# Expert results by indirect DMA to a table of rows, instead of a scatter on TensorE for each expert

## The reference

```python
N_EXPERTS, TOP_K, D_FF_EXPERT = 8, 2, 2816
logits = xt @ router
top_val, top_idx = lax.top_k(logits, TOP_K)
top_w = jax.nn.softmax(top_val, axis=-1)
gates = sum(one_hot(top_idx) * top_w)             # (tokens, experts)
for e in range(N_EXPERTS):
    out = out + gates[:, e:e + 1] * ((silu(xt @ wg[e]) * (xt @ wu[e])) @ wd[e])
x = layer_norm(ALPHA * x + out, ln2_g, ln2_b)
```

## Time and profile before

| | |
|---|---|
| Median of 3 runs | 2399.91 us (2394.61 to 2399.92) |
| The profiled execution, whole | 2399.19 us |
| Its span, first to last instruction | 2397.4 us |
| TensorE busy (matmuls) | 2368.5 us, 99% |
| DVE busy | 1722.4 us, 72% |
| ACT busy | 1450.2 us, 60% |
| GpSimd (POOL) busy | 80.4 us, 3% |
| HBM read, written | 551.10 MB, 1.05 MB |
| Mean granted TensorE clock | 0.999 of full |

### The profile page before, as it was taken

How to read it: one execution, slowest core, us unless ns; L and a number is a source line. 1 busy time by engine, 2 the same in 40 slices (tenths; PEclk the granted TensorE clock), 3 DMA queues, 4 the chain that set the end, 5 groups by cost and what they waited for, 6 DMA issues and landing times. The chain is left out here.

```text
span 2397.4 us, 31585 instructions
## 1 busy us (share of the span) xinstructions
PE 2368.5 (99%) x12354; PEld 1993.1 (83%) x12354; DVE 1722.4 (72%) x1921; ACT 1450.2 (60%) x1674; POOL 80.4 (3%) x114
## 2 busy tenths in 40 slices
PE   9999999999999999999999999999999999999998
PEld 7889978788888888888878788888888888887887
DVE  5665466899898899889986755666656766568565
ACT  6454454688888888888856544454444544456442
POOL 0000010000000000000001100000000000003000
PEclk9999999999999999999999999999999999999999
DMA  8255552699999999899955355443555255453552
GB/s 314 94 198 204 189 202 75 262 366 361 352 361 357 344 366 371 338 358 363 359 192 206 129 207 185 180 177 116 207 186 194 87 191 191 186 189 124 189 190 104
DMA packets 81806, 555.18 MB, mean 232 GB/s; under 512 B 11072, under 2 KB 11840, under 8 KB 16192
## 3 DMA queue, kind: packets, MB, share of 16 engines
q1 hardware_dynamic: 81600, 552.19, 61.7%
HBM read 551.10 MB, written 1.05 MB: 230 GB/s over the span
## 5 line engine op out<-in xcount | busy, mean ns | idle before, releaser
L2140 DVE TENSOR_TENSOR wlo<-raw,whi 128x2048 fp32r<-128x2048 f32 x484 | 1105.3, 2295 | 432.7 <-ACT whi L1690 431.6
L1690 ACT ACTIVATE whi<-raw 128x2048 fp32r<-128x2048 f32 x487 | 932.6, 1928 | 538.5 <-PE bank L896 139.0
L818 PE MATMUL bank<-whi,xt 128*128 128x512 f32 (+1 forms) x1056 | 311.1, 379 | 2.4 <-DVE xt L2157 1.3
L1237 PE MATMUL bank<-whi,xt 128*128 128x512 f32 (+1 forms) x768 | 222.4, 374 | 1.5 <-DVE e_hf L2786 1.4
L818 PEld LDWEIGHTS bank<-whi,xt 128*128 128x128 f32 x1056 | 189.4, 188 | 39.9 <-issue 3.3
L1052 PE MATMUL bank<-xt,whi 128*128 128x512 f32 x768 | 209.1, 394 | 0.0
L818 PE MATMUL bank<-wlo,xt 128*128 128x512 f32 (+1 forms) x528 | 197.6, 374 | 0.0
L896 PE MATMUL bank<-whi,h_hi 128*128 128x512 f32 x596 | 184.9, 391 | 0.0
L896 PE MATMUL bank<-whi,h_lo 128*128 128x512 f32 x596 | 183.9, 390 | 0.0
L896 PE MATMUL bank<-wlo,h_hi 128*128 128x512 f32 x596 | 183.8, 390 | 0.0
L1237 PEld LDWEIGHTS bank<-whi,xt 128*128 128x128 f32 x768 | 138.5, 188 | 26.4 <-DVE e_hf L2786 1.9
(11 more groups left out here) (346 smaller groups left out, 3700.6 us busy)
## 6 DMA issues: line engine op xcount, KB each, us to landing
raw<-in_units SPq DMA_DIRECT2D x509, 1024.0 KB, 5.0
gain<-in_ln_g SPq DMA_DIRECT2D x4, 512.0 KB, 6.8
gain<-in_ln_b SPq DMA_DIRECT2D x4, 512.0 KB, 8.5
gain<-in_attn_norm_g SPq DMA_DIRECT2D x4, 512.0 KB, 6.0
gain<-in_mlp_norm_g SPq DMA_DIRECT2D x4, 512.0 KB, 6.1
toep<-in_toeplitz SPq DMA_DIRECT2D x2, 768.0 KB, 10.0
cst<-in_cst SPq DMA_DIRECT2D x1, 1120.0 KB, 18.9
x<-in_x SPq DMA_DIRECT2D x4, 256.0 KB, 6.0
```

The source lines that it names most:

```text
L818: mm = pe.matmul(proj_bank(l, c, t)[:, 0:width], a[:, kx, t * P:(t + 1) * P], b[:, k, :], start=(kx == 0 and i == 0), stop=(kx == KT - 1 a ...
L1237: mm = pe.matmul(bank[b][:, 0:width], a[:, kx, :], w[:, k, :], start=(kx == 0 and i == 0), stop=(kx == KT - 1 and i == 2))
L1690: act.activation(whi[u % NH][:, :], raw[u % NR][:, :], ACT.Copy).then_inc(hi_ready[u % NR], 2)
L2140: dve.tensor_tensor(wlo[u % NR][:, :], raw[u % NR][:, :], whi[u % NH][:, :].bitcast(F32), ALU.subtract).then_inc(lo_ready[u % NR], 2)
```

## The change

The results of experts 0 to 6 are no longer scattered by a matmul. ACT copies the four result banks to a plain float32 tile (`give_plain_result`; `xt_rows` and `odd_rows` lie on the same bytes as `xt` and the odd token tiles), and GpSimd issues two indirect DMAs an expert, one for each tile of 128 slots. They write slot rows of 4 KB to a table `rows` in HBM: row 2 x token + choice, where choice is 1 if the expert is the token's second. Slots without a token get an index of at least 1024, past the bounds, and are not written. `index_rows` on TensorE finds the row of each slot: four matmuls of the permutation with `row_base` (eight columns), in place of `turn_perm`; DVE adds 1024 and casts (`index_of_rows`). In the last expert, before the loads of group 45, SyncE waits until all stores have landed and reads the table back, 1 MB for each tile of tokens; DVE combines the two rows of each token with their softmax weights in groups 3 and 4 (`add_rows`, three instructions a tile), in place of the single add in group 2. The last expert keeps its scatter. An all-zero input `no_rows` is copied to the table in layer 0, after the small loads. `y` is no longer cleared.

```diff
+            xt_rows = sb("xt_rows", [P, 2, 2, D], scope=plain)
+                odd_rows = sb("odd_rows", [P, 2, 2, D], scope=plain)
@@ SyncE, load_experts and layer 0
+                    if g == n - NG + 3:
+                        sp.wait_ge(rows_stored, 32 * (N_EXP - 1))
+                        back = rows.rearrange("(t p w) d -> t p w d", t=NT, w=2)
+                        for t in range(NT):
+                            sp.dma_start(rows_of(t), back[t]).then_inc(rows_back, 16)
                     if g < n:
                         load_units(PLAN.gate[1][g])
...
                     small()
+                    sp.dma_start(rows, A["no_rows"]).then_inc(rows_cleared, 16)
@@ GpSimd
-                            pool.memset(y[:, t, half * 512:(half + 1) * 512], 0.0).then_inc(added, 1)
+                    pool.wait_ge(rows_cleared, 16)
+                    for e in range(N_EXP - 1):
+                        pool.wait_ge(map_ready, e + 1)
+                        pool.wait_ge(ye_hi_ready, 4 * e + 4)
+                        for st in range(NT):
+                            pool.indirect_dma_start(
+                                rows, bass.IndirectOffsetOnAxis(ap=row_of[:, e, st:st + 1], axis=0),
+                                plain_results(e)[:, st], None, bounds_check=2 * S - 1,
+                                oob_is_err=False).then_inc(rows_stored, 16)
@@ TensorE
+            def index_rows(e):
+                third_bank_free(e)
+                if e < 2:
+                    pe.wait_ge(wide_placed, e + 1)
+                for st in range(NT):
+                    for t in range(NT):
+                        mm = pe.matmul(bank[3][:, st * 8:(st + 1) * 8], perm[:, e // 2 % 2, t, st, e % 2], row_base[:, t],
+                                       start=(t == 0), stop=(t == 1))
+                mm.then_inc(slots_mapped, 1)
...
                 def between(i, place):
-                    if i == 1 and place == 0 and e:
-                        narrow_or_wide(n_before, scatter, e - 1)
                     if i == 2 and place == 0:
-                        turn_perm(e)
+                        (index_rows if n_next is not None else turn_perm)(e)
...
                         if g == 1:
-                            pe.wait_ge(perm_t_ready, e + 1)
+                            pe.wait_ge(map_ready, e + 1)
...
+                        if n_next is not None:
+                            pe.wait_ge(map_ready, e + 1)
                         next_own(gate_of, 0)
@@ ACT
                 def take_tokens(p, g):
                     act.wait_ge(gathered, p * 8 + (g + 1))
+                    if p and g == 4:
+                        act.wait_ge(rows_stored, 32 * (2 * p - 1))
...
+                def give_plain_result(e):
+                    wait_used(act, PLAN.down[1][e * NG + NG - 1][-1])
+                    if e:
+                        act.wait_ge(rows_stored, 32 * e)
+                    for b in range(4):
+                        act.activation(plain_results(e)[:, b // 2, b % 2 * 512:(b % 2 + 1) * 512], bank[4 + b][:, :],
+                                       ACT.Copy).then_inc(ye_hi_ready, 1)
@@ DVE
+                def index_of_rows(e):
+                    dve.wait_ge(slots_mapped, e + 1)
+                    dve.tensor_scalar(row_of[:, e], bank[3][:, 0:16].rearrange("p (s e) -> p s e", s=NT)[:, :, e],
+                                      float(NO_ROW), None, ALU.add).then_inc(map_ready, 1)
+                def add_rows(t):
+                    dve.wait_ge(rows_back, 32)
+                    link(dve.tensor_scalar(y[:, t], rows_of(t)[:, 0], topf[:, t, 6:7], None, ALU.mult))
+                    link(dve.scalar_tensor_tensor(out=y[:, t], in0=rows_of(t)[:, 1], scalar=topf[:, t, 7:8],
+                                                  in1=y[:, t], op0=ALU.mult, op1=ALU.add))
+                    link(dve.scalar_tensor_tensor(out=x[:, t], in0=x[:, t], scalar=ALPHA, in1=y[:, t], op0=ALU.mult,
+                                                  op1=ALU.add))
...
+                for t in range(NT):
+                    dve.tensor_scalar(row_base[:, t], cst[:, C_IOTA:C_IOTA + 8], topf[:, t, 1:2],
+                                      cst[:, C_ROW + t:C_ROW + t + 1], ALU.is_equal, ALU.add)
                 for e in range(2):
                     place_tokens(e, slice(1, 2), wide_placed)
...
-                    if i == 1 and e:
-                        add_result(e - 1, 0)
...
+                    if i == 2 and e < N_EXP - 1:
+                        index_of_rows(e)
...
-                    if i == 1 and e:
-                        add_result(e - 1, 1)
-                    if i == 0 and e:
-                        split_result(e - 1)
-                    if e == N_EXP - 1 and i == 2:
-                        dve.wait_ge(added, 4 * N_EXP)
-                        for t in range(NT):
-                            ins = dve.scalar_tensor_tensor(out=x[:, t], in0=x[:, t], scalar=ALPHA, in1=y[:, t],
-                                                           op0=ALU.mult, op1=ALU.add)
-                        link(ins)
+                    if e == N_EXP - 1 and i in (3, 4):
+                        add_rows(i - 3)
```

More of the change, by code:

```diff
@@ L169, with build @@
 PI_SAFE = 3.1415925
-def build(nc, A, out):
+def build(nc, A, out, rows):
     with ExitStack() as ctx:
@@ L1321, in fold_unit @@
                                                stop=(i == NG - 1 and f == 1 and p == 2))
-                                if i == NG - 1 and not wide and kk == 0 and p == 0 and half == 0:
+                                if e == N_EXP - 1 and i == NG - 1 and not wide and kk == 0 and p == 0 and half == 0:
                                     mm.then_inc(res_minus, 1)
@@ L1335, in fold_hidden @@
                 pe.wait_ge(low_a, g + 1)
-                if i == 0:
-                    pe.wait_ge(added, 4 * e + 2)
+                if i == 0 and e:
+                    pe.wait_ge(ye_hi_ready, 4 * e - 2)
                 for j in range(len(PLAN.down[1][g])):
@@ L1341, in fold_hidden @@
                     mm.then_inc(done, 1)
-                if i == NG - 1 and wide:
-                    subtract_high(e)
             def fold_last_groups(e, wide):
@@ L1387, in narrow_or_wide, with expert @@
                     what(args[0], True, *args[1:])
[L1389 removed]
+            def expert(e, n, n_next):
                 def own(what, i):
@@ L2001, in between @@
                 def between(e, i, place):
-                    if i == 2 and place == 0:
+                    if i == 2 and place == 0 and e == N_EXP - 1:
                         take_perm(e)
@@ L2808, in split_result @@
                                           ALU.subtract).then_inc(ye_lo_ready, 1)
-                def add_result(e, t):
-                    for half in range(2):
-                        c = slice(half * 512, (half + 1) * 512)
-                        dve.wait_ge(scattered, e * 4 + (2 * t + half + 1))
-                        dve.wait_ge(added, e * 4 + (2 * t + half + 1) if e else 4 + 2 * t + half)
-                        dve.scalar_tensor_tensor(out=y[:, t, c], in0=bank[4 + 2 * t + half][:, :],
-                                                 scalar=gw[:, t, e:e + 1], in1=y[:, t, c], op0=ALU.mult,
-                                                 op1=ALU.add).then_inc(added, 1)
                 dve.wait_ge(got["iota"], 16)
@@ L3094 @@
     out = nc.dram_tensor("out", (1, S, D), F32, kind="ExternalOutput").ap()
-    build(nc, aps, out)
+    rows = nc.dram_tensor("expert_rows", (2 * S, D), F32, kind="Internal").ap()
+    build(nc, aps, out, rows)
     r = run(nc, [{"in_" + n: a for n, a in arrays.items()}], core_ids=[0])
```

102 lines of the change are left out of this document (56 added, 46 removed).

## The result

The changed kernel takes **2420.53 us**, median of 4 (2418.54 to 2422.36), against 2399.91 (2394.61 to 2400.70): ratio 1.0090, 95% interval 1.0073 to 1.0108. It is slower by 20.6 us; the forecast was 2399, its range 2390 to 2410. The profiled execution took 2418.54 us around a span of 2416.7.

The account below looks back on a forecast made before the run. TensorE was taken to bound the experts, with splits and loads close behind. The terms -13.5 + 1.6 + 0.4 + 0.5 + 6.5 + 1.9 + 2.4 = -0.2 gave 2399 us from 2399.19; range 2390 to 2410.

Parts of the forecast that it names:

- the stores, costed at nothing: Experts: fourteen indirect DMAs on GpSimd, 0.7 us of DMA time in 94 per expert, covered by idle DMA time; cost 0.
- TensorE's terms: Experts: seven scatters removed -13.5 us, index_rows +1.6, row_base operations ahead of first splits +0.4, gather 1 waiting for DVE +0.5.
- the sign "under 0.3 us": Experts 1, 3 and 5: gather 1 would wait under 0.3 us for DVE, as a check of the forecast.
- Rival C: Every expert: loads become the bound, the 13.5 us are not won, last expert's costs remain; 2410 us, chance 0.10.
- The read back: Start of expert 7: SyncE's wait and two 1 MB read backs delay unit gate 45, stalling TensorE; +6.5 us (2.9 to 12.9).
- R: Time from the end of expert 6's last down group until the stores are seen; 7.7 us (4.1 to 14.1).
- Rival B: Wait before gate 45: indirect DMAs and landing take over 13 us, stall passes 14; 2407 to 2415 us, chance 0.12.
- The clock: Expert 7: the stall drops TensorE's granted clock to 0.50, costing +1.9 us (0 to 4).
- The end of expert 7: Groups 3 and 4: add_rows on DVE makes the last group's low part late; +2.4 us (0 to 5).
- The clearing: Layer 0: 2 MB from HBM to HBM on SyncE's queue at 73 us, hidden by a pause; cost 0.
- rival D: Layer 0: the clearing blocks the loads by running on one engine; about 2440 us, chance 0.03.
- Rival E: DVE keeps GpSimd out of SBUF: each indirect DMA first waits out a split; R 12.3, 2404 us, chance 0.08.

Follow-up runs that it names:

- kernel 5: Experiment 4's kernel without any transfer of rows: no stores, read back or row additions, so results of experts 0 to 6 are missing; 2388.54 us, ratio 0.9959.
- 10: Experiment 4's kernel with the stores kept, but the 2 MB read back and row additions left out; 2394.77 us, ratio 0.9987.
- 15: 10 with another slot table from the host, so that an expert's tokens take the even partitions first; 2389.81 us, ratio 0.9960.
- Experiment 4: experiment 3's kernel with the wait for the last stores and the read back issued by GpSimd instead of SyncE; 2402.57 us, ratio 1.0014.
- 17: Experiment 8's kernel with the spread slots (even partitions first), computing everything; 2394.50 us, ratio 0.9986.
- Experiment 8: Experiment 4's kernel with add_rows after groups 2 and 3 instead of 3 and 4, and index_of_rows one split earlier; 2400.13 us, ratio 1.0008.
- experiment 1: Kernel before the change with the tile of constants 32 unused columns (128 bytes a partition) larger, nothing else; 2418.77 us, ratio 1.0081.
- experiment 3: Changed kernel with tiles in their old places: row numbers in unused columns of cst, the two small new tiles behind xw_lo; 2407.43 us, ratio 1.0039.

## Why the prediction was wrong

**The step that failed** is one that the sum does not have: it takes every stage but the experts as unchanged. I looked at what the new columns of `cst` hold, and not at what they push along. Measured, the places are 11 to 13 us of the 20.6: by the marks 9.5 in the five dense stages, where the forecast has nothing, and 1.6 in the experts (5.1 in experts 0 to 6, less 3.5 that expert 7 takes longer without them). With the old places the kernel is at 2407.43, inside the range but 8.4 above the forecast. The second step that failed is the stores, costed at nothing: 6.2 us. The other terms can be held against the trace one by one.

**TensorE's terms: right.** The forecast was -13.5 + 1.6 + 0.4 + 0.5 = -11.0 without costs of transfers and tail; kernel 5 has 2388.54 - 2398.46 = -9.9. `index_rows` took 0.49 us in the timeline (589.79 to 590.28; 0.44 forecast). Each of experts 1 to 5 in kernel 5 gains 1.8 us between the two turns around its scatter, expert 6 2.2; 1.93 was forecast. Gather 1 waited 0.93 us in expert 1 and 0.35 in expert 3 for `row_of`, 1.3 in all (0.5 forecast, range 0 to 4; the sign "under 0.3 us" did not hold).

**The stores, costed at nothing: mis-sized.** "0.7 us of DMA time in 94, which the 6 to 8% of idle DMA time covers" failed at the cover. The earlier trace rows has shares of 0.98 and 0.92, so that 2 to 8% were idle and not 6 to 8, but a mean share said little either way. The stores cost 6.2 us over seven experts, 0.9 each, and 5.0 of it went with other partitions. Rival C had the sign of this, weights that come late, but not the size or the cause: TensorE did not lose what the scatters gave (kernel 5), and 8 MB of extra copies cost only 7 to 8 us, so it was not for want of bandwidth. That the rows fell to one half of the DMA engines is the reading that fits 10 and 15; it is not shown.

**The read back: right in mechanism, and nearly in size.** R was 7.7 forecast and 6.7 measured (GpSimd's two issues 0.96 us each with 0.30 between, 1.3 each forecast); gate 45 landed at 17.7 instead of 18.8. The second store was seen 2.5 us after its issue began (1157.68 to 1160.21), on queues that SyncE's wait had let run nearly dry (DMA share 0.31 from 1158 to 1160). It is the tile of slots 128 to 255, which holds no token here; the first, which holds the rows, had landed by then, at most 3.8 us after its issue began (1156.41). The Trainium skill's 2.0 us plus the bytes over 436 GB/s ("DMA: Bandwidth & Descriptors", Anatomy of one DMA) gives as an estimate 2.0 for the second and 2.6 for the first (0.26 MB), near what the trace has. Over all the stores, most of them beside the weights, the median was 6.1 to 6.4 us. TensorE's need for it is at 16.5 by the forecast's reckoning, its start was at 22.2, of which 5.22 are visible idle. With the clock, the interval from the turn of group 1 to that of group 2 (18.63 before, less 1.93 for the scatter, 24.68 after) lengthened by 8.0 us, against 6.5 + 1.9 = 8.4. The chain that set it: copies, stores, landing, two MB ahead of a weight unit. Experiment 4 confirms the place: another queue for the read back, 4.9 us less. What it does not give back is the cost of 2 MB among the weights and of the additions: between 15 and 17, which differ by these and by the place of `index_of_rows`, lie 4.7 us. Rival B, a wait of over 14 us here, did not come.

**The clock: right.** It was at 0.50 within about 3.5 us of TensorE's falling idle, and back 4.5 us after TensorE began again at 1175.69. In that stretch matmuls are 0.43 us apart instead of 0.23; 4.5 us at half speed cost some 2.2, where 1.9 was forecast.

**The end of expert 7: right in mechanism.** 2.4 forecast, TensorE's wait is 2.85, and from the turn of the last group to the mark at the end of the experts it takes 3.3 us longer; with the old places 5.0. From the turn of group 2 on it is 2.1. Experiment 8 turned 3.72 us of wait into 0.98.

**The clearing** was hidden as forecast: SyncE's queue was at the next unit load at 79.07, before it 80.09. The dense stage of layer 0 did lengthen, by 1.1 us, but so it does in experiment 1, which has no clearing: that is the places, and not rival D. Rival E does not show: the two issues took 0.96 us each.

**Put together.** The one trace of the changed kernel can be added up by itself, from GpSimd's marks and the turns of the hidden tile, as a difference to the kernel before (us):

| Stretch | Forecast | Measured |
|---|---|---|
| Start of the experts to the turn of group 1 of expert 7 | -9.1 | +2.5 |
| From there to the turn of group 2 | +6.5 | +6.05 |
| From there to the end of the experts | +2.4 | +2.1 |
| Outside the experts | 0 | +8.6 |
| Span | -0.2 | +19.3 |

In the first row -9.1 is six scatters (-11.6) and what TensorE and DVE get in their place (+2.5); in the second +6.5 is the wait and the clock less the seventh scatter. The trace is 11.6 us above it: some 5.2 are the places (the estimate of experiment 3), and the 6.4 left are close to the 6.2 that the stores cost in 10 against 5. Without any transfer of rows, kernel 5 is at -8.6 there. So the forecast is right where it looked, to within half a microsecond in each of the two rows of expert 7 and, against kernel 5, in the first, and it is off by the places (5.2 and 8.6) and the stores (6.4). Some of this closeness is luck: with the old places (kernel 3) the two stretches of expert 7 are +7.2 and +4.5.

## What to carry to other kernels

Before a sum is made, list which tiles move in SBUF, not only which instructions change: 32 columns that nobody reads cost the kernel before 20 us, as much as the whole change. Put new constants where room is left, or pad so that later tiles move by a multiple of 256 bytes, and compare the mean of one instruction in a stage that the change does not touch; it is a cheap control. A mean DMA share under one hides nothing by itself: small indirect stores with all their valid rows in the first half of the partitions cost 0.9 us each time beside a stream of weights, and spread rows 0.2, one plain store of 64 rows 0.1 (both by medians, and one kernel with spread rows does not fit). And a transfer that must wait for others does not belong in the queue that feeds the bound engine.

## What the runs showed of the hardware that was not expected

- A 512-column fp32 matmul whose stationary tile begins 128 bytes off its old place takes 394 to 396 ns instead of 389 to 391 in the records; 48 of them took 11.2 us instead of 10.9. Shifts of 256 and 512 bytes change nothing, and in the changed kernel the two odd tiles, shifted by a multiple of 256, kept their speed. Which tile it is to be aligned with (the moving ones, `whi` and `wlo`, did not move) was not tried.
- Seven times 64 rows stored by indirect DMA cost 6.2 us from the first half of the partitions and 1.3 from all (2389.81 against 2388.54); as plain stores of 64 rows from the first half, 0.5 (2389.08).
- Around TensorE's wait for gate 45 (1168 to 1180 us) the DMA engines moved 424 to 428 GB/s, where the earlier trace rows has at most 374 at a share of 0.98: a share near one is not the ceiling of what they can move.
- The granted clock came back from 0.50 about 4.5 us after TensorE's start.
